# Placing the two operands of the full-width products at agreeing SBUF addresses in a hybrid decoder trunk

## The chip, the cores and the metric

One Trainium2 chip, one of its cores. The time is the device time of one execution of the whole program, in microseconds (us); lower is better. Three runs of the kernel before gave 2153.06, 2153.92 and 2160.28 us, median 2153.92.

## What is computed

The reference is a two-layer decoder trunk over 1024 tokens of width 1024, with 16 learned meta tokens in front (1040 positions). Layer 0 is a state-space mixer with a gated output projection and a mixture of experts (MoE); layer 1 is sliding-window attention over a shared K/V and a second MoE. Everything is in float32.

```python
h = h + s5_mixer(rmsnorm(h), ...)            # ends in z @ w_glu: 1040 x 1024 by 1024 x 2048
h = h + hier_moe(rmsnorm(h), ...)            # 32 experts, each 1024 -> 512 (gate, up) -> 1024 (down)
k, v = split(rmsnorm(h) @ w_kv + b_kv)       # 1024 x 512
q = rmsnorm(h) @ w_q + b_q                   # 1024 x 1024
h = h + (attention(q, k, v, sinks) @ w_o + b_o)
h = h + hier_moe(rmsnorm(h), ...)
return rmsnorm(h)[meta tokens dropped]
```

## The kernel before

**Split products.** A float32 product with a large weight is made of three TensorE products. Each operand is split into a part `hi` (rounded to the fp32r format by ScalarE) and a rest `lo` (VectorE subtracts), and TensorE adds hi x hi, lo x hi and hi x lo into one PSUM bank. One such product has a stationary operand of 128 x 128, loaded by its own LDWEIGHTS, and a moving operand of 128 x 512 that is streamed from SBUF while the next product's stationary operand is being loaded. These are the full-width products of the title. TensorE does them back to back, in five places:

- the mixer's projection, lines 810 to 812 (`products` in `phase_mixer`): four quarters of the weight by nine token tiles by eight chunks by three, 864 products (96 of them for the meta tile, which has 16 stationary columns). Stationary: `z_hi`, `z_lo`. Moving: the weight, `w_hi`, `w_lo`;
- the MoE of each layer, lines 1876 to 1878 (`products` in `phase_moe`): 32 tiles of 128 rows, one per expert here, with 48 products for gate and up and 24 for down, 2304 for each layer. Stationary: `x_hi`, `x_lo`, then `h_hi`, `h_lo`. Moving: the expert's weight in `hi` and `lo`. Between them stand 8 transposes of the gathered rows (`xg`, line 1861) and 4 of the hidden tile (line 1870);
- the K/V/Q projections, line 1094 (`project_pe`): 480 products of 512 columns with the weight stationary and `prj_x_hi`, `prj_x_lo` moving; V is made the other way round, in products of 256 columns, and the meta rows in short ones;
- the output projection of attention, lines 2235 to 2237 (`project` in `phase_attend`): 384 products in bursts of six between the other steps of attention, the last 48 nearly together. Stationary: `o_hi`, `o_lo`. Moving: `wo_hi`, `wo_lo`.

**The order of work.** Each engine runs its own list; semaphores join them. In an MoE layer SP loads three 2 MB weights per expert into six buffers (`raw`), ScalarE makes `hi`, VectorE `lo`, three slots each, and TensorE sends `w_used` when a slot is done. Rows come by an indirect DMA from GpSimd.

|---|---|---|---|
| mixer | `w_hi`, `w_lo`: 128 | `z`: 128, rows of 1040 words, so chunk c lies 64 c further, tokens 64 further | 64, 128, 192, 0, repeated over chunks |
| MoE, layer 0 | `hi` (57568), `lo` (82144): 224 | `x_hi` (157664), `x_lo`, `h_hi`, `h_lo`: 224 | 0 throughout |
| K/V/Q | `prj_x`: 224, rows of 1040 words, so chunk c lies 64 c further | `w_hi`, `w_lo`: 224 | 0, 192, 128, 64, repeated over chunks |
| attention output | `wo_hi`, `wo_lo`: 32 | `o_hi`, `o_lo`: 192 | 160 throughout |
| MoE, layer 1 | `hi` (57568), `lo` (82144): 224 | `x_hi` (154368), `x_lo`, `h_hi`, `h_lo`: 0 | 32 throughout |

The two MoE layers run the same instructions of the same function; the addresses behind the router's tables differ because layer 0 has nine token tiles and layer 1 eight, and layer 0 also holds the biases of the projections.

Of the kernel before, what the change touches and what calls it, by code (L numbers as in the profile page):

```python
# [9 lines left out]
F32R = mybir.dt.float32r  # L10
# [9 lines left out]
SEQ = 1024  # L20
N_META = 16
T_ALL = SEQ + N_META
P = 128
DC = D // P
XT = SEQ // P
# [24 lines left out]
RAW_AT = 229344 - 6 * 8192  # L50
TILE_ORDER = (XT,) + tuple(range(XT))

def tile_rows(i):

    return P if i < XT else N_META
# [33 lines left out]
def phase_mixer(nc, t):  # L90
# [9 lines left out]
    CB = DC  # L100
    NQ = 4
    QW = D // NQ
    BANKS = 6
    RW = G * NCH
    h = t["h"]
    w_glu = t["ssm_w_glu"][0].rearrange("(c p) (v q m) -> p c v q m", c=DC, v=2, q=NQ)
    xm_dram, h_dram, zm_dram = t["xm_dram"], t["h_dram"], t["zm_dram"]
    with ExitStack() as ctx:
        def sb(name, shape, dt=F32):
            return ctx.enter_context(nc.sbuf_tensor("mix_" + name, shape, dt))  # L110

        def region(name, words):

            at = -(-nc.sbuf_base // 32) * 32
            return at, sb(name, [P, words])

        def over(name, shape, at, dt=F32):

            return nc.alloc_sbuf_tensor_at("mix_" + name, shape, dt, offset=at)
# [5 lines left out]

        r1_at, r1 = region("r1", RW)
        v_re, v_im = (r1[:, q * L * JC:(q + 1) * L * JC].rearrange("p (j k c) -> p j k c", k=L, c=C) for q in range(2))
        xm_sq = r1[0:N_META, 0:D]
        st_n = r1[:, :].rearrange("p (a n) -> p a n", n=NCH)

        r2_at, r2 = region("r2", RW)
        xt = r2[:, 0:L * D].rearrange("p (g q c) -> p g q c", g=G, c=C)
        st_a = r2[:, :].rearrange("p (i e a b) -> p i e a b", e=NE, i=BLK, a=8)
        w_raw = r1[:, 0:4 * D].rearrange("p (f c v m) -> p f c v m", f=2, c=DC // 2, v=2)

        r3_at, r3 = region("r3", RW)
        xs = r3[:, 0:L * D].rearrange("p (q d) -> p q d", q=L)
        xm2 = r3[0:2, 0:L * D].rearrange("p (g q c) -> p g q c", g=G, c=C)
        hbuf = r3[0:C, RW // 2:RW // 2 + HB * 4 * HW].rearrange("p (b g m) -> p b g m", b=HB, g=4)
        tm = r3[:, :].rearrange("p (g m) -> p g m", g=G)  # L140

        r4_at, r4 = region("r4", RW)
        sq = r4[:, 0:L * D].rearrange("p (q d) -> p q d", q=L)
        uc = r4[:, :].rearrange("p (g n) -> p g n", g=G)

        s1_at, s1 = region("s1", 4 * D)
        b_raw = s1[:, 0:2 * JC].rearrange("p (x j c) -> p x j c", x=2, c=C)
        c_raw = s1[:, 2 * JC:4 * JC].rearrange("p (x a m) -> p x a m", x=2, m=S)
# [12 lines left out]
        z1 = s1[:, Z0:Z0 + 8 * NCH].rearrange("p (b s n) -> p b s n", b=2, s=4)  # L161
        z_cb = s1[:, Z0 + 8 * NCH:Z0 + 8 * NCH + D].rearrange("p (s g c) -> p s g c", s=L, c=C)

        z_hi, z_lo = (over(f"z_{x}", [P, CB, T_ALL], at, F32R) for x, at in (("hi", r4_at), ("lo", r3_at)))
        HALF = 4 * RW // 2
        w_hi = [over(f"w_hi{b}", [P, DC, 2 * QW], at, F32R) for b, at in enumerate((r2_at, r1_at + HALF))]
        w_lo = [over(f"w_lo{b}", [P, DC, 2 * QW], at, F32R) for b, at in enumerate((r2_at + HALF, s1_at))]
# [72 lines left out]
        def _(sp):  # L240
# [41 lines left out]
            for i in range(NT):  # L282
                n = tile_rows(i)
                src = t["x"][0, i * P:(i + 1) * P, :] if i < XT else t["meta_tokens"]
                sp.dma_start(h[0:n, i, :], src).then_inc(h_in, 16)
# [50 lines left out]
        def _(act):  # L336
# [107 lines left out]
            for q in range(NQ):  # L444
                if q + 1 < NQ:
                    for half in range(2):
                        split_w(q + 1, half)
                if q == 0:
                    act.wait_ge(zm_in, 32)
                    nc.scalar.copy(z_hi[:, :, 0:N_META], zmr[:].rearrange("p b n s -> p b (n s)")).then_inc(zm_hi_done, 1)  # L450
                for i in range(NT):
                    k, n = q * NT + i, tile_rows(i)
                    act.wait_ge(acc_done, k + 1)
                    if k >= 2:
                        act.wait_ge(val_done, k - 1)
                    nc.scalar.activation(sig[0:n, k % 2, :], acc(k)[0:n, QW:2 * QW], ACT.Sigmoid).then_inc(sig_done, 1)

        @block.vector
        def _(dve):
# [201 lines left out]
            for q in range(NQ):  # L661
                if 1 <= q < NQ - 1:
                    for half in range(2):
                        split_w(q + 1, half)
                for i in range(NT):
                    k, n = q * NT + i, tile_rows(i)
                    dve.wait_ge(sig_done, k + 1)
                    if k >= 2:
                        dve.wait_ge(h_done, k - 1)
                    V.tensor_tensor(val[0:n, k % 2, :], acc(k)[0:n, 0:QW], sig[0:n, k % 2, :],  # L670
                                    ALU.mult).then_inc(val_done, 1)
                    dve.wait_ge(val_done, k + 1)
                    hq = h[0:n, i, q * QW:(q + 1) * QW]
                    V.tensor_tensor(hq, hq, val[0:n, k % 2, :], ALU.add).then_inc(h_done, 1)
# [177 lines left out]
KV = N_KV * DH  # L852
NEG = -1e30
SC_W = N_META + 2 * P
TOK = XT * P + N_META
K_META = tuple((3 * m + 1) * P + m * N_META for m in range(3))
K_W = XT * P + len(K_META) * N_META

# [14 lines left out]
def projections(nc, t, sb, sem, ident, mhalf, ss, rstd, ps_x, acc):  # L873
# [18 lines left out]
    bk = sb("prj_bk", [P, K0])  # L892
    bq = sb("prj_bq", [P, DC])
    bv = sb("prj_bv", [P, KV])
    x_at = -(-nc.sbuf_base // 32) * 32
    x_hi, x_lo = (nc.alloc_sbuf_tensor_at(f"prj_x_{x}", [P, DC, TOK], F32R, offset=x_at + q * 4 * DC * TOK)
                  for q, x in enumerate(("hi", "lo")))
    yc = nc.alloc_sbuf_tensor_at("prj_yc", [P, N_YC, 2, D], F32, offset=t["qkv_at"])
    xn = nc.alloc_sbuf_tensor_at("prj_xn", [P, 2, D], F32, offset=t["qkv_end"])
# [21 lines left out]
        return max(k for k, job in enumerate(jobs) if job[0] == (n if n >= K0 else 0)) + 1  # L921

    def split(x, i):
        return x[:, :, i * P:i * P + tile_rows(i)]

    def turned(j):
        return ps_x[j % 2].rearrange("p (c m) -> p c m", c=DC)[:, :, 0:tile_rows(TILE_ORDER[j])]
# [41 lines left out]
    def project_act(act):  # L969
# [15 lines left out]
        def hi_part(j):  # L985
            act.wait_ge(xt_mm, j + 1)
            A.copy(split(x_hi, TILE_ORDER[j]), turned(j)).then_inc(xt_hi, 1)
# [79 lines left out]
    def project_pe(pe):  # L1067
        T = nc.tensor

        def turn(j):  # L1070
            i, n = TILE_ORDER[j], tile_rows(TILE_ORDER[j])
            pe.wait_ge(xn_done, j + 1)
            if j >= 2:
                pe.wait_ge(xt_lo, j - 1)
            for c in range(DC):
                last = T.transpose(ps_x[j % 2][:, c * P:c * P + n],
                                   xn[0:n, j % 2, :].rearrange("p (m c) -> p c m", c=DC)[:, c, :], ident[0:n, 0:n])
            last.then_inc(xt_mm, 1)

        def product(k):  # L1080
            n, at, m = jobs[k]
            if k >= 4:
                pe.wait_ge(acc_free, k - 3)
            for c in range(DC):
                xh, xl = x_hi[:, c, at:at + m], x_lo[:, c, at:at + m]
                if n < K0:
                    wh, wl = w_hi[:, 0:K0, c, :], w_lo[:, 0:K0, c, :]
                    out = acc[k % 4][0:m, 0:KV].rearrange("p (b f) -> p b f", b=K0)
                    pairs = ((xh, wh), (xl, wh), (xh, wl))
                else:  # L1090
                    wh, wl = w_hi[:, n % W_KV, c, :], w_lo[:, n % W_KV, c, :]
                    out, pairs = acc[k % 4][:, 0:m], ((wh, xh), (wh, xl), (wl, xh))
                for s, (stationary, moving) in enumerate(pairs):
                    last = T.matmul(out, stationary, moving, start=(c == 0 and s == 0), stop=(c == DC - 1 and s == 2))
            last.then_inc(acc_done, 1)

        for j in range(NT):
            turn(j)
            if j >= 1 and j < NT - 1:
                pe.wait_ge(xt_lo, j)  # L1100
                product(j - 1)
        for k in range(NT - 2, len(jobs)):
            n, at, m = jobs[k]
            if n < K0:
                pe.wait_ge(xt_lo, NT - 1 if k == NT - 1 else NT)
            elif n >= Q0:
                pe.wait_ge(w_lo_done, n - Q0 + 1)
            product(k)
# [4 lines left out]
def phase_moe(nc, t, layer, out=None):  # L1113
# [27 lines left out]
    with ExitStack() as ctx:  # L1141
        def sb(name, shape, dt=F32):
            return ctx.enter_context(nc.sbuf_tensor(f"moe{layer}_{name}", shape, dt))
# [6 lines left out]
        hi, lo = (sb(x, [P, 3, KC * F], F32R) for x in ("hi", "lo"))  # L1150
# [7 lines left out]
        if not last_layer:  # L1158
            project_sp, project_pool, project_act, project_dve, project_pe = projections(
                nc, t, sb, sem, ident, mhalf, ss, rstd, (ps_xt, ps_y), (ps_g, ps_u, ps_ht, ps_m))  # L1160
# [44 lines left out]
        gi = sb("gi", [P, 1], I32)  # L1205
        unit = sb("unit", [P, 2])
        si = sb("si", [P, 1], I32)
        xg = sb("xg", [P, D])
        x_hi, x_lo = (sb(f"x_{x}", [P, DC, P], F32R) for x in ("hi", "lo"))
        silu = sb("silu", [P, F])  # L1210
# [717 lines left out]
def phase_attend(nc, t):  # L1928
# [16 lines left out]
    with ExitStack() as ctx:  # L1945
        def sb(name, shape, dt=F32):
            return ctx.enter_context(nc.sbuf_tensor("att_" + name, shape, dt))

        def ps(name, shape):
            return ctx.enter_context(nc.psum_tensor("att_" + name, shape, F32))  # L1950
# [6 lines left out]
        own_t = sb("own_t", [P, P])  # L1957
        sinks = sb("sinks", [P, N_HEADS])
        raw = sb("raw", [P, 4, HALF])
        wo_hi, wo_lo = (sb(f"wo_{x}", [P, DC, D], F32R) for x in ("hi", "lo"))  # L1960
        sm = sb("sm", [P, 2, ROW])
        nm = sb("nm", [P, 2, H2])
# [4 lines left out]
        p_own = sb("p_own", [P, 2, H2 * P])  # L1967
        v_step = sb("v_step", [P, 2, KV])
        v_meta = sb("v_meta", [3 * N_META, KV])
        o_hi, o_lo = (sb(f"o_{x}", [P, 2, DC, P], F32R) for x in ("hi", "lo"))  # L1970
        ps_s = ps("ps_s", [P, 4, 512])
        ps_t = ps("ps_t", [P, 2, 512])
# [333 lines left out]
```

## Time and profile before

| | us |
|---|---|
| median of three runs | 2153.92 |
| lowest and highest run | 2153.06, 2160.28 |
| the profiled execution, whole | 2154.48 |
| its span, first to last instruction | 2152.4 |
| TensorE matmuls busy | 1959.0 |
| TensorE weight loads busy | 1573.1 |
| VectorE busy | 1580.2 |
| ScalarE busy | 1251.7 |
| GpSimd busy | 374.3 |
| mean granted TensorE clock, share of full speed | 0.960 |

TensorE is the busiest engine. Its matmuls are pipelined, each being recorded as 0.39 us long while the next begins about 0.23 us after it, so the time of a row of products is read from their starts, not from their durations.

### The profile page before, as it was taken

How to read it: one execution, taken by the hardware profiler on the slowest of the kernel's cores; microseconds unless marked ns; L12 is line 12 of the kernel's file. 1: busy time of each engine (PE TensorE's matmuls, PEld its weight loads, DVE VectorE, ACT ScalarE, POOL GpSimd, SP SyncE). 2: the span in 40 equal slices, each digit the busy share in tenths (PEclk: the TensorE clock that was granted, in tenths of full speed). 3: DMA queues.
4: the chain of work that ended last, by engine and by line, in shares of the span. 5: the costliest groups of instructions: out<-in, count | busy, mean ns of one | idle time of the engine just before them, and what ended most of it. 6: DMA issues, size and time to landing. Idle time of an engine off the chain costs nothing. (4 is left out here: it accounts for less than half of the span.)

```text
span 2152.4 us, 31937 instructions
## 1 busy us (share of the span) xinstructions
PE 1959.0 (91%) x10762; PEld 1573.1 (73%) x10762; DVE 1580.2 (73%) x1767; ACT 1251.7 (58%) x1532; POOL 374.3 (17%) x673
## 2 busy tenths in 40 slices
PE   4959999859999999999699999995899999999991
PEld 3648777748888888888588766664788888888870
DVE  8996321468999999989752376656688888888885
ACT  6614210427777777777530265534577777777771
POOL 1000000401222222221233000003122111122214
PEclk9979999979999999999799999998899999999995
DMA  4174200439999999999612110007599999999976
GB/s 102 26 73 158 91 1 1 169 131 366 385 384 379 380 380 382 383 389 387 230 53 56 46 45 2 1 1 257 189 358 353 374 378 381 386 384 384 381 309 244
DMA packets 136045, 504.69 MB, mean 234 GB/s; under 512 B 38466, under 2 KB 68498, under 8 KB 84754
## 3 DMA queue, kind: packets, MB, share of 16 engines
q1 hardware_dynamic: 114658, 468.71, 59.5%
q0 software_dynamic: 18432, 33.86, 4.1%
q10 hardware_dynamic: 2880, 1.12, 0.4%
q8 instruction: 47, 0.77, 0.2%
q14 instruction: 28, 0.23, 0.0%
HBM read 488.47 MB, written 47.32 MB: 249 GB/s over the span
## 5 line engine op out<-in xcount | busy, mean ns | idle before, releaser
L1713 DVE TENSOR_TENSOR moe_lo<-moe_raw,moe_hi 128x2048 fp32r<-128x2048 f32 x378 | 860.8, 2291 | 102.4 <-ACT moe_hi L1488 99.3
L1488 ACT CAST moe_hi<-moe_raw 128x2048 fp32r<-128x2048 f32 x374 | 712.9, 1915 | 139.8 <-PE moe_ps_g L1878 67.0
L1876 PE MATMUL moe_ps_g<-moe_hi,moe_x_hi 128*128 128x512 f32 x512 | 209.0, 408 | 4.9 <-DVE moe_lo L1713 3.0
L1876 PE MATMUL moe_ps_y<-moe_hi,moe_h_hi 128*128 128x512 f32 x512 | 207.0, 404 | 3.8 <-DVE moe_h_lo L1729 3.8
L1878 PE MATMUL moe_ps_g<-moe_lo,moe_x_hi 128*128 128x512 f32 x512 | 203.0, 396 | 0.0
L1877 PE MATMUL moe_ps_g<-moe_hi,moe_x_lo 128*128 128x512 f32 x512 | 202.7, 396 | 0.0
L1878 PE MATMUL moe_ps_y<-moe_lo,moe_h_hi 128*128 128x512 f32 x512 | 202.0, 395 | 0.0
L1877 PE MATMUL moe_ps_y<-moe_hi,moe_h_lo 128*128 128x512 f32 x512 | 201.8, 394 | 0.0
L1878 PE MATMUL moe_ps_u<-moe_lo,moe_x_hi 128*128 128x512 f32 x512 | 201.2, 393 | 0.0
L1876 PE MATMUL moe_ps_u<-moe_hi,moe_x_hi 128*128 128x512 f32 x512 | 200.8, 392 | 0.0
L1877 PE MATMUL moe_ps_u<-moe_hi,moe_x_lo 128*128 128x512 f32 x512 | 200.8, 392 | 0.0
L1495 ACT CAST moe_x_hi<-moe_ps_xt 128x1024 fp32r<-128x1024 f32 x62 | 63.0, 1015 | 114.7 <-PE moe_ps_xt L1861 114.7
L1876 PEld LDWEIGHTS moe_ps_g<-moe_hi,moe_x_hi 128*128 128x128 f32 x512 | 98.3, 192 | 25.1 <-DVE moe_lo L1713 3.4
L1876 PEld LDWEIGHTS moe_ps_y<-moe_hi,moe_h_hi 128*128 128x128 f32 x512 | 96.7, 189 | 23.5 <-DVE moe_lo L1713 4.1
L1878 PEld LDWEIGHTS moe_ps_g<-moe_lo,moe_x_hi 128*128 128x128 f32 x512 | 97.3, 190 | 22.6
L1878 PEld LDWEIGHTS moe_ps_y<-moe_lo,moe_h_hi 128*128 128x128 f32 x512 | 96.6, 189 | 22.1
L1877 PEld LDWEIGHTS moe_ps_g<-moe_hi,moe_x_lo 128*128 128x128 f32 x512 | 97.7, 191 | 19.6
L1878 PEld LDWEIGHTS moe_ps_u<-moe_lo,moe_x_hi 128*128 128x128 f32 x512 | 96.1, 188 | 21.6
L1876 PEld LDWEIGHTS moe_ps_u<-moe_hi,moe_x_hi 128*128 128x128 f32 x512 | 96.1, 188 | 21.6
L1877 PEld LDWEIGHTS moe_ps_u<-moe_hi,moe_x_lo 128*128 128x128 f32 x512 | 96.1, 188 | 21.6
L1405 POOL COPY moe_si<-moe_idx_out 128x1 int32 x64 | 49.9, 779 | 353.9 <-ACT moe_y L1508 353.9
L1877 PEld LDWEIGHTS moe_ps_y<-moe_hi,moe_h_lo 128*128 128x128 f32 x512 | 96.8, 189 | 19.5
(463 smaller groups left out, 3745.3 us busy)
## 6 DMA issues: line engine op xcount, KB each, us to landing
moe_raw<-moe_w_gate SPq DMA_DIRECT2D x128, 1024.0 KB, 6.9
moe_raw<-moe_w_up SPq DMA_DIRECT2D x128, 1024.0 KB, 7.9
moe_raw<-moe_w_down SPq DMA_DIRECT2D x128, 1024.0 KB, 7.4
mix_r<-ssm_w_glu SPq DMA_DIRECT2D x16, 512.0 KB, 5.4
xn_dram<-moe_work SPq DMA_DIRECT2D x16, 512.0 KB, 6.4
prj_yc<-y_dram SPq DMA_DIRECT2D x8, 1024.0 KB, 7.0
moe_raw<-y_dram SPq DMA_DIRECT2D x8, 1024.0 KB, 11.7
mix_r<-x SPq DMA_DIRECT2D x8, 512.0 KB, 5.3
```

Of the source, the lines that this page charges most:

```text
L1405: G_.tensor_copy(dst[:, :], idx[:, bass.ds(tile, 1)]).then_inc(ix_step, 1)
L1488: A.copy(hi[:, slot(number, k), :], raw[:, k, :]).then_inc(hi_done, 1)
L1495: A.copy(x_hi[:, :, :].rearrange("p c m -> p (c m)"), ps_xt[:, :]).then_inc(xt_hi, 1)
L1713: V.tensor_tensor(lo[:, slot, :], raw[:, k, :], hi[:, slot, :].bitcast(F32), ALU.subtract).then_inc(lo_done, 1)
L1876: T.matmul(out, x_h, w_h, start=first, stop=False)
L1877: T.matmul(out, x_l, w_h, start=False, stop=False)
L1878: return T.matmul(out, x_h, w_l, start=False, stop=final)
```

## The change

No instruction is added, removed or reordered. Only addresses change.

- `aligned(base, like)` gives the next address at or above `base` that is a multiple of 32 and, if `like` is given, agrees with it modulo 256. `lead` declares an unused tile of so many words that the next tile begins at such an address.
- Mixer: each row of `z_hi` and `z_lo` gets 48 unused words in front (`Z_PAD`), so that rows are 1088 words (17 x 256 bytes) apart and the tokens begin at 128 modulo 256, as the weights do. The regions under them grow by 1536 bytes each. The meta columns (16 of them, before the tokens) then lie 64 below the weights modulo 256 in every chunk.
- K/V/Q: `prj_x_hi` and `prj_x_lo` keep 1024 token columns; the 16 meta columns move to tiles of their own. Their start is made to agree with `RAW_AT` (224), where it already is.
- MoE: `xg` is led to the residue of `t["qkv_at"]`, 224. In layer 0 that skips nothing; in layer 1 it skips 224 bytes, and `xg`, `x_hi`, `x_lo`, `silu`, `hid`, `h_hi`, `h_lo` and `y` all move from 0 to 224.
- Attention: `o_hi` and `o_lo` move by 96 bytes, from 192 to 32.

```diff
+def aligned(base, like=None):
+    at = -(-base // 32) * 32
+    return at if like is None else at + (like - at) % 256
+
+def lead(nc, sb, like):
+    skip = aligned(nc.sbuf_base, like) - aligned(nc.sbuf_base)
+    if skip:
+        sb("lead", [P, skip // 4])
...
+    Z_PAD = 48
...
+        sb("r3_more", [P, CB * Z_PAD])
         r4_at, r4 = region("r4", RW)
...
+        sb("r4_more", [P, CB * Z_PAD])
         s1_at, s1 = region("s1", 4 * D)
...
-        z_hi, z_lo = (over(f"z_{x}", [P, CB, T_ALL], at, F32R) for x, at in (("hi", r4_at), ("lo", r3_at)))
+        z_hi, z_lo = (over(f"z_{x}", [P, CB, Z_PAD + T_ALL], at, F32R)[:, :, Z_PAD:]
+                      for x, at in (("hi", r4_at), ("lo", r3_at)))
...
-    x_at = -(-nc.sbuf_base // 32) * 32
-    x_hi, x_lo = (nc.alloc_sbuf_tensor_at(f"prj_x_{x}", [P, DC, TOK], F32R, offset=x_at + q * 4 * DC * TOK)
+    x_at = aligned(nc.sbuf_base, RAW_AT)
+    m_at = x_at + 2 * 4 * DC * SEQ
+    x_hi, x_lo = ((nc.alloc_sbuf_tensor_at(f"prj_x_{x}", [P, DC, SEQ], F32R, offset=x_at + q * 4 * DC * SEQ),
+                   nc.alloc_sbuf_tensor_at(f"prj_xm_{x}", [P, DC, N_META], F32R, offset=m_at + q * 4 * DC * N_META))
                   for q, x in enumerate(("hi", "lo")))
...
-                xh, xl = x_hi[:, c, at:at + m], x_lo[:, c, at:at + m]
+                xh, xl = columns(x_hi, c, at, m), columns(x_lo, c, at, m)
...
         si = sb("si", [P, 1], I32)
+        lead(nc, sb, t["qkv_at"])
         xg = sb("xg", [P, D])
...
+        wo_at = aligned(nc.sbuf_base)
         wo_hi, wo_lo = (sb(f"wo_{x}", [P, DC, D], F32R) for x in ("hi", "lo"))
...
+        lead(nc, sb, wo_at)
         o_hi, o_lo = (sb(f"o_{x}", [P, 2, DC, P], F32R) for x in ("hi", "lo"))
```

## Rows read from the trace of the kernel before

**Rows 1.** Windows view, one stage each: us, busy us (x instructions) by engine, PEclk, DMA share, GB/s

```profile
196.00:398.00 202.00, 201.33 (x885) 154.00 (x883) 47.50 (x82) 30.94 (x52) 0.00 (x0) 1.00 0.17 56
464.00:1037.00 573.00, 566.16 (x2660) 473.93 (x2661) 508.62 (x288) 446.85 (x318) 117.67 (x214) 0.99 0.96 367
1094.00:1216.00 122.00, 121.15 (x572) 99.95 (x570) 33.18 (x55) 8.42 (x8) 35.04 (x16) 1.00 0.16 44
1247.00:1455.00 208.00, 206.06 (x1444) 133.34 (x1442) 131.47 (x469) 106.15 (x449) 9.96 (x53) 1.00 0.03 9
1515.00:2105.50 590.50, 583.98 (x2680) 478.22 (x2680) 506.78 (x285) 448.68 (x317) 114.65 (x215) 0.99 0.93 354
```

**Rows 2.** Waits view of TensorE, 1510 to 2106 us, longest: total us, times, longest us

```profile
PE moe_ps_ht L1870 <- DVE moe_hid L1725: 3.0, 1, 3.0
```

**Rows 3.** Waits view of all engines, layer 0's MoE, 520 to 1030 us

```profile
DVE moe_lo L1713 <- ACT moe_hi L1488: 34.6, 87, 0.4
ACT moe_hi L1488 <- PE moe_ps_y L1878: 23.4, 29, 0.8
```

**Rows 4.** Timeline view of TensorE: start us, us; eight transposes, layer 0, 27 tiles apart

```profile
530.74 1.04 PE L1861 MATMUL moe_ps_xt<-moe_ident,moe_xg 128*128 128x128 f32 x8
...
1010.08 1.04 PE L1861 MATMUL moe_ps_xt<-moe_ident,moe_xg 128*128 128x128 f32 x8
```

**Rows 5.** Timeline view of TensorE, the same transposes in layer 1, 27 tiles apart

```profile
1582.83 1.05 PE L1861 MATMUL moe_ps_xt<-moe_ident,moe_xg 128*128 128x128 f32 x8
...
2073.25 1.05 PE L1861 MATMUL moe_ps_xt<-moe_ident,moe_xg 128*128 128x128 f32 x8
```

**Rows 6.** Timeline view of TensorE, layer 0: two products of "up", twelve apart

```profile
915.86 0.39 PE L1876 MATMUL moe_ps_u<-moe_hi,moe_x_hi 128*128 128x512 f32 x1
...
918.58 0.39 PE L1876 MATMUL moe_ps_u<-moe_hi,moe_x_hi 128*128 128x512 f32 x1
```

**Rows 7.** Timeline view of TensorE, layer 1: two products of "up", twelve apart

```profile
1813.36 0.40 PE L1876 MATMUL moe_ps_u<-moe_hi,moe_x_hi 128*128 128x512 f32 x1
...
1816.16 0.40 PE L1876 MATMUL moe_ps_u<-moe_hi,moe_x_hi 128*128 128x512 f32 x1
```

**Rows 8.** Timeline view of TensorE, the mixer's projection: one pass over four chunks

```profile
353.05 0.40 PE L810 MATMUL mix_pst<-mix_w_hi,mix_z_hi 128*128 128x512 f32 x1
...
355.13 0.40 PE L810 MATMUL mix_pst<-mix_w_hi,mix_z_hi 128*128 128x512 f32 x1
355.37 0.39 PE L811 MATMUL mix_pst<-mix_w_hi,mix_z_lo 128*128 128x512 f32 x1
...
355.83 0.40 PE L810 MATMUL mix_pst<-mix_w_hi,mix_z_hi 128*128 128x512 f32 x1
```

**Rows 9.** Timeline view of TensorE, K/V/Q: two products, twelve apart

```profile
1131.59 0.39 PE L1094 MATMUL moe_ps_g<-prj_x_hi,w_hi 128*128 128x512 f32 x1
...
1134.37 0.39 PE L1094 MATMUL moe_ps_g<-prj_x_hi,w_hi 128*128 128x512 f32 x1
```

**Rows 10.** Timeline view of TensorE, attention: four intervals inside a burst of six

```profile
1325.04 0.39 PE L2236 MATMUL att_ps_y<-att_wo_hi,att_o_lo 128*128 128x512 f32 x1
...
1325.97 0.40 PE L2237 MATMUL att_ps_y<-att_wo_lo,att_o_hi 128*128 128x512 f32 x1
```

**Rows 11.** Timeline view of TensorE, attention's last half projection, 23 intervals

```profile
1448.93 0.39 PE L2235 MATMUL att_ps_s<-att_wo_hi,att_o_hi 128*128 128x512 f32 x1
...
1454.30 0.39 PE L2237 MATMUL att_ps_s<-att_wo_lo,att_o_hi 128*128 128x512 f32 x1
```

**Rows 12.** Timeline view of TensorE, layer 0: second to eighth product behind transposes

```profile
910.62 0.39 PE L1877 MATMUL moe_ps_g<-moe_hi,moe_x_lo 128*128 128x512 f32 x1
...
912.01 0.39 PE L1877 MATMUL moe_ps_g<-moe_hi,moe_x_lo 128*128 128x512 f32 x1
```

**Rows 13.** Timeline view of TensorE, layer 0: five products at the start of "down"

```profile
904.67 0.39 PE L1877 MATMUL moe_ps_y<-moe_hi,moe_h_lo 128*128 128x512 f32 x1
...
905.60 0.39 PE L1878 MATMUL moe_ps_y<-moe_lo,moe_h_hi 128*128 128x512 f32 x1
```

More of the change, by code:

```diff
@@ L854 @@
 SC_W = N_META + 2 * P
-TOK = XT * P + N_META
 K_META = tuple((3 * m + 1) * P + m * N_META for m in range(3))
@@ L923, in split, with columns @@
     def split(x, i):
-        return x[:, :, i * P:i * P + tile_rows(i)]
+        return x[0][:, :, i * P:(i + 1) * P] if i < XT else x[1][:, :, :]
+    def columns(x, c, at, m):
+        return x[0][:, c, at:at + m] if at < XT * P else x[1][:, c, :]
     def turned(j):
```

## The prediction

> **What bounds the kernel now.** I read the windows view by stage first. In the five stages that hold full-width products TensorE is busy for 201.33 of 202, 566.16 of 573, 121.15 of 122, 206.06 of 208 and 583.98 of 590.5 us; no other engine comes near except VectorE in the MoE layers (508.62 and 506.78) [rows 1]. The waits view says the same from the other side: in all of layer 1's MoE the longest wait of TensorE is one of 3.0 us at the start [rows 2], while in layer 0's steady part TensorE has none; there ScalarE waits 29 times for TensorE to give a slot back, and VectorE for ScalarE [rows 3]. No engine waits for a weight transfer. So these stages, about 1,695 us of the 2152.4, end when TensorE's list ends, and the list's length is the number of products times the interval between their starts. The change alters no instruction, so the whole question is that interval. The timeline's starts give it; durations do not.
>
> **The interval depends on the addresses.** The kernel before holds a comparison of its own: the same function runs as two MoE layers. The instructions and the tile sizes are the same; what differs is that the stationary operands agree with the moving ones modulo 256 bytes in layer 0 and lie 32 bytes off in layer 1. From one tile's transposes to those 27 tiles later layer 0 takes 1010.08 - 530.74 = 479.34 us, 17.753 a tile [rows 4]; layer 1 takes 2073.25 - 1582.83 = 490.42, 18.164 a tile [rows 5]. Inside a tile, twelve products of "up" take 2.72 us in layer 0, 226.7 ns each [rows 6], and 2.80 us in layer 1, 233.3 ns each [rows 7]. The clock is granted in full in both. The gap of 6.6 ns on 72 products would be 0.48 us a tile; the tiles differ by 0.41, because in layer 0 the first products behind the transposes are not yet at the low interval: six intervals take 1.39 us, 231.7 each [rows 12], so 6 x 5.0 ns twice a tile, 0.06 us, are not gained.
>
> The other stages fit. The mixer, whose difference walks through 64, 128, 192, 0, takes 2.78 us for twelve, 231.7 each [rows 8]; K/V/Q, which walks the other way, 2.78 as well [rows 9]. Attention's last run, 160 off throughout, takes 5.37 us for 23, 233.5 each [rows 11]. So a difference that merely stays the same doesn't bring 226.7 (32 and 160 don't); of the constant ones seen, only 0 does. What I can't see is a stage with difference 0 on residues other than 224, or whether 0 in the mixer and K/V/Q does what it does in the MoE.
>
> The Trainium skill speaks against the change: "SBUF — State Buffer", "Who interferes with whom", gives TensorE two independent read ports, one for the moving operand and one for weight loads, and says that TensorE waits for nobody. By that rule addresses would make no difference, and the sum would be zero. The trace doesn't agree, with 17.753 against 18.164 us for one and the same list.
>
> **The change, part by part.**
>
> *MoE, layer 1.* The lead of 224 bytes puts its stationary operands where layer 0 has theirs modulo 256. I take layer 0's time for it: 32 tiles x (18.164 - 17.753) = 13.1 us. Bounds: 0, if the difference between the layers isn't the address, and 32 x 72 x 6.6 ns = 15.2 us, if the slow start behind the transposes went too. What would be late next is the feed (ScalarE's `hi`, VectorE's `lo`, the weight transfers), and layer 0 already runs it at 17.753 with TensorE never waiting [rows 1, 3, 4]. Its DMA share is 0.96 against 0.93, so there is little room below that pace, but none is needed.
>
> *Mixer.* 768 of the 864 products come to difference 0. At 231.7 - 226.7 = 5.0 ns each that is 3.8 us. The four meta tiles stay off (by 192) and I leave their 96 products at today's interval; behind each, six intervals of relocking as in rows 12 cost 0.03 us, 0.1 in all. I take 3.7 us, bounds 0 and 864 x 5.0 ns = 4.3. Nothing else there is near TensorE's 201.33 us: VectorE has 47.50 and ScalarE 30.94 [rows 1].
>
> *K/V/Q.* 480 products of 512 columns x 5.0 ns = 2.4 us, less 0.1 for restarts behind the short meta products: 2.3. The 256-column products of V and the meta products I leave as they are; if V's 192 moved by 5 ns either way, it would be 1.0 us. GpSimd's 35.04 us in 122 leaves it ahead [rows 1].
>
> *Attention.* The bursts of six are too short: four intervals inside one take 0.93 us [rows 10], and layer 0's four at the same place behind transposes, with difference 0, take 0.93 too [rows 13]. Only the nearly continuous end gains: some 40 intervals x (233.5 - 226.7) = 0.3 us. Bounds 0 and, if the 56 bursts ran at 226.7 at once, 56 x 4 x 5.8 ns = 1.3 us more.
>
> *Layer 0's MoE, the copies, the DMAs.* `xg` doesn't move in layer 0. ScalarE's and VectorE's writes of `z` and `prj_x` go to rows a little further apart or closer, and no row shows such a step to cost anything; if it did, their idle time in these stages would hide it. The unused tiles are neither written nor read. All other tiles of the mixer move by 1536 or 3072 bytes, multiples of 256. I take nothing.
>
> Sum: 13.1 + 3.7 + 2.3 + 0.3 = 19.4 us. The profiled execution took 2154.48 us, 2.08 more than its span, so 2135.1; the median lies 0.56 below that execution, so 2134.5.
>
> **What else moves.** Stages begin up to 19 us earlier, and with them the stretches at half clock between stages. The two MoE layers lose about a hundredth of their time to such stretches (PEclk 0.99) [rows 1], some 6 us each, and the three runs differ by up to 7.2 us. One such stretch more or less is about 3 us. I put +-4 us on the median for it.
>
> **Rivals.**
>
> *Only layer 1's MoE gains.* Agreement modulo 256 might be enough only with residue 224, or only in an order of operands as in the MoE; mixer and K/V/Q would go on at 231.7. For it: no row shows them at difference 0 for long, and the mixer has agreeing products that still take long (next rival). 2134.5 + 6.3 = 2140.8.
>
> *The layers differ for another reason.* A loop that is paced by something else, the transfers for instance, would show the same two periods, and the skill's rule on the two ports leads here. Against it: TensorE doesn't wait, and the mixer and K/V/Q differ from both within one loop, chunk by chunk. No change, 2153.9.
>
> *Agreement is the collision.* If two streams that start on the same residue meet in the same part of the memory, agreeing is the worst case, and layer 0 escapes it only by a fixed lag. In the mixer the interval from 355.13 to 355.37, where a moving operand at 128 meets the load of a stationary one at 128, is 240 ns by the timeline, longer than its neighbours [rows 8]. The place would be the mixer's and K/V/Q's lists, which have no gap in which such a lag could form. If every agreeing product took some 236 ns (240 as printed, in steps of 10, over the 231.7 mean), mixer and K/V/Q would lose 1,248 x 4.3 ns = 5.4 us, and layer 1, if caught as well, 2304 x 2.7 ns = 6.2 us: 2165.5. It decides once agreeing products average over 233.3 ns in layer 1; layer 0, all agreeing, averages 226.7 [rows 6], which speaks strongly against it.
>
> **How the numbers follow.** Forecast as summed: 0.78, with its own range 2130.5 to 2138.5. Only layer 1: 0.11. No difference: 0.06. Slower by collision: 0.05. The range reaches from 2130, where the meta tiles, attention's bursts and V also gain, to 2143, which takes in the second case with a half-clock stretch on top. A difference under 0.3%, about 6.5 us, is what a measurement can't tell from none. Faster by more than that: 0.88; within it: 0.07; slower: 0.05.
>
> **What would show it.** In the profile after, twelve products of "up" in layer 1 should take 2.72 us and its tiles 17.75; twelve in the mixer and in K/V/Q 2.72 instead of 2.78, with the meta tiles unchanged; attention's last 23 intervals 5.21 instead of 5.37; layer 0 nothing. The forecast is wrong if layer 1 still takes 18.16 (the reason isn't the address), if TensorE begins to wait in it (the feed bounds), or if the mixer's intervals stay mixed (agreement isn't enough).

## The result, and the profile after

The median went from 2155.19 us (2153.06 to 2160.28, four runs) to 2137.44 us (2136.98 to 2138.15, four runs): ratio 0.9913, 95% interval 0.9897 to 0.9930. A second comparison of the same two kernels gave 2155.73 and 2138.82 us (2137.52 to 2142.09), ratio 0.9924, 0.9904 to 0.9943. The forecast was 2134.5, its range 2130 to 2143. The profiled execution of the kernel after took 2138.15 us and has a span of 2136.2, 16.2 less than before. In its line numbers the mixer's products are 827 to 829, K/V/Q's 1115, the MoE's 1898 to 1900 with the transposes on 1883, attention's 2259 to 2261.

Windows view of the kernel after, the five stages (us, busy us and instructions of PE, PEld, DVE, ACT and POOL, PEclk, DMA share, GB/s); it answers to [rows 1]:

```profile
195.70:394.40 198.70, 197.99 (x887) 154.14 (x885) 47.52 (x82) 31.13 (x52) 0.00 (x0) 1.00 0.17 57
462.00:1035.00 573.00, 566.60 (x2662) 474.50 (x2662) 508.32 (x287) 447.11 (x317) 117.24 (x213) 0.99 0.96 367
1092.00:1213.60 121.60, 120.45 (x571) 101.20 (x570) 32.91 (x55) 8.41 (x8) 34.89 (x16) 0.99 0.16 44
1245.00:1451.20 206.20, 204.32 (x1436) 133.16 (x1436) 130.83 (x468) 105.30 (x447) 9.89 (x53) 1.00 0.03 9
1511.00:2089.50 578.50, 571.74 (x2679) 478.20 (x2677) 506.15 (x284) 446.80 (x317) 120.78 (x215) 0.99 0.94 361
```

The mixer's window is 3.3 us shorter and layer 1's 12.0, with the work in them as before. TensorE still fills every window; the other engines' busy times are the same within 2 us, apart from GpSimd's 6 us more in layer 1.

Timeline view of TensorE, the kernel after (start us, duration us, line, operation): eight transposes in layer 1, 27 tiles apart, as [rows 5]; two products of "up" in layer 1, twelve apart, as [rows 7]:

```profile
1576.69 1.04 PE L1883 MATMUL moe_ps_xt<-moe_ident,moe_xg 128*128 128x128 f32 x8
...
2056.03 1.04 PE L1883 MATMUL moe_ps_xt<-moe_ident,moe_xg 128*128 128x128 f32 x8
...
1802.71 0.39 PE L1898 MATMUL moe_ps_u<-moe_hi,moe_x_hi 128*128 128x512 f32 x1
...
1805.43 0.39 PE L1898 MATMUL moe_ps_u<-moe_hi,moe_x_hi 128*128 128x512 f32 x1
```

27 tiles take 479.34 us, 17.753 each, layer 0's period to the last digit [rows 4]; twelve products take 2.72 us, 226.7 ns each.

The same view in the mixer (two products of a token tile, twelve apart, as [rows 8]; then two of the meta tile, 16 stationary columns, twelve apart), in K/V/Q (as [rows 9]) and over attention's last 23 intervals (as [rows 11]):

```profile
350.33 0.39 PE L827 MATMUL mix_pst<-mix_w_hi,mix_z_hi 128*128 128x512 f32 x1
...
353.05 0.39 PE L827 MATMUL mix_pst<-mix_w_hi,mix_z_hi 128*128 128x512 f32 x1
...
241.21 0.40 PE L827 MATMUL mix_psr<-mix_w_hi,mix_z_hi 128*16 128x512 f32 x1
...
243.99 0.40 PE L827 MATMUL mix_psr<-mix_w_hi,mix_z_hi 128*16 128x512 f32 x1
...
1127.74 0.39 PE L1115 MATMUL moe_ps_m<-prj_x_hi,w_lo 128*128 128x512 f32 x1
...
1130.46 0.39 PE L1115 MATMUL moe_ps_m<-prj_x_hi,w_lo 128*128 128x512 f32 x1
...
1445.36 0.39 PE L2259 MATMUL att_ps_s<-att_wo_hi,att_o_hi 128*128 128x512 f32 x1
...
1450.58 0.39 PE L2261 MATMUL att_ps_s<-att_wo_lo,att_o_hi 128*128 128x512 f32 x1
```

Mixer and K/V/Q now take 2.72 us for twelve instead of 2.78; attention 5.22 for 23 instead of 5.37; the meta tile stays at 2.78.

Where the 16.2 us are. Each stage is measured from the start of its first product or transpose to the start of its last, before against after; "second" is the profile of the same kernel in the second comparison (span 2135.8). Rounding leaves 0.1 in a column:

| | forecast | after | second |
|---|---|---|---|
| mixer | -3.7 | -3.5 | -3.5 |
| MoE, layer 0 | 0 | +0.2 | +0.2 |
| K/V/Q | -2.3 | -0.3 | -0.4 |
| attention | -0.3 | -1.0 | -1.0 |
| MoE, layer 1 | -13.1 | -11.6 | -14.1 |
| between the stages | 0 | -0.1 | +2.1 |
| sum | -19.4 | -16.2 | -16.7 |

Two terms fell short, K/V/Q and, in the first profile, layer 1. In both places there is a stretch at half clock inside the list of products. Timeline view of TensorE, the kernel after, K/V/Q behind K's 24 short meta products:

```profile
1109.50 0.26 PE L1115 MATMUL moe_ps_m<-prj_xm_hi,w_lo 128*128 128x16 f32 x1
1109.62 0.30 PE L1115 MATMUL moe_ps_m<-prj_xm_hi,w_hi 128*128 128x16 f32 x1
...
1111.19 0.63 PE L1115 MATMUL moe_ps_g<-prj_x_hi,w_lo 128*128 128x512 f32 x1
1111.62 0.63 PE L1115 MATMUL moe_ps_g<-prj_x_hi,w_hi 128*128 128x512 f32 x1
```

Windows view of TensorE (us, busy us and instructions, PEclk, DMA share, GB/s): the kernel after, at that place and in the last tile of layer 1:

```profile
1109.70:1113.10 3.40, 3.40 (x11) 0.50 0.35 104
1113.10:1116.50 3.40, 3.40 (x16) 1.00 0.17 51
...
2078.00:2082.50 4.50, 2.58 (x14) 1.00 0.00 0
2082.50:2085.90 3.40, 3.40 (x10) 0.50 0.16 58
```

The kernel before, at K/V/Q's place, and the kernel after in its second profile, at layer 1's:

```profile
1109.40:1112.80 3.40, 3.40 (x29) 1.00 0.05 12
1112.80:1116.20 3.40, 3.40 (x17) 1.00 0.53 154
```

```profile
2078.40:2081.80 3.40, 2.60 (x14) 1.00 0.00 0
2081.80:2085.20 3.40, 2.27 (x10) 1.00 0.03 10
2085.20:2088.60 3.40, 3.40 (x16) 1.00 0.11 43
```

Full-width products stand 0.43 us apart instead of 0.227: 3.4 us at 1.2 GHz instead of 2.4 do the work of 1.7. Of the 2.0 us that K/V/Q misses, list by list, 1.6 are this stretch. The lists with V's 192 products of 256 columns are 0.2 longer than before, and so is the list of V's short meta products ahead of them, which differs by more than that from run to run. The 480 products of 512 columns themselves give back what was forecast: where no stretch stands in them, their four lists take 108.93 us against 111.24 before, 2.3 less (run "walk" below).

Layer 1 misses 1.5 us in the first profile, where its last tile holds such a stretch. The second profile has none there, and its 14.1 exceeds the term because the stretch near the start of the layer is 3.4 us long (granted clock 0.50 from 1529.8 to 1533.2 us) instead of 6.8 (before, from 1531.5 to 1538.3).

### The profile page after: what moved, and what is told of

The parts are those of the page before. It is cut to its first block and busy times, and to the rows that moved or that the text cites. A ratio compares the mean times of both kernels' runs of the same rounds, so it can differ in the third digit from the quotient of the medians.

```text
span 2136.2 us, 31937 instructions
## 1 busy us (share of the span) xinstructions
PE 1941.3 (91%) x10762; PEld 1575.1 (74%) x10762; DVE 1580.2 (74%) x1767; ACT 1249.3 (58%) x1532; POOL 376.4 (18%) x673
## 6 DMA issues: line engine op xcount, KB each, us to landing
moe_raw<-y_dram SPq DMA_DIRECT2D x8, 1024.0 KB, 11.6
```

## The experiments

Intervals below are means of start-to-start times of full-width products at full clock, more than ten products behind the last other instruction, without the few over 300 ns, unless rows are shown. Runs given with one time are single runs; what they show is read from their intervals, not from that time.

**Which half does what.** The kernel before with nothing but layer 1's lead:

```diff
+        lead(nc, sb, t["qkv_at"])
         xg = sb("xg", [P, D])
```

> The kernel before with one part of the change: the 224 bytes of lead in layer 1's MoE. Theory (agreement modulo 256 sets the interval): a tile of layer 1 takes 17.75 us instead of 18.16, twelve products of 'up' 2.72 instead of 2.80, the mixer and K/V/Q stay at 2.78, and the time is 13 us below before (ratio 0.994). Rival 'another reason' (the two MoE layers differ for something other than the address): no change, ratio 1.000.

Measured: 2145.25 us against 2157.8, ratio 0.9944 (0.9925 to 0.9963). Timeline view of TensorE in this run, layer 1's transposes 27 tiles apart, then its waits view for the layer (total us, times, longest us):

```profile
1580.62 1.04 PE L1875 MATMUL moe_ps_xt<-moe_ident,moe_xg 128*128 128x128 f32 x8
...
2064.30 1.04 PE L1875 MATMUL moe_ps_xt<-moe_ident,moe_xg 128*128 128x128 f32 x8
```

```profile
PE moe_ps_xt L1875 <- DMA moe_xg<-xn_dram,moe_gi: 2.2, 1, 2.2
```

The 483.68 us hold one late gather of rows: two tiles took 18.01 and 21.83 us, 4.34 more than their neighbours, with a half-clock stretch behind the wait of 2.2. The rest is 479.34 again, 17.75 a tile. All other stages are as before. So 224 bytes of unused words give layer 1 its whole gain per tile.

The counterpart is the changed kernel without that lead:

```diff
-        lead(nc, sb, t["qkv_at"])
         xg = sb("xg", [P, D])
```

> The changed kernel without its lead in layer 1's MoE, so only mixer, K/V/Q and attention are placed. Theory: twelve products take 2.72 us in the mixer and in K/V/Q, a tile of layer 1 still 18.16, and the time is 6 us below before (ratio 0.997). Rival 'only layer 1 gains': the mixer and K/V/Q stay at 2.78 and the time is that of before.

Measured: 2150.88 us, ratio 0.9969 (0.9959 to 0.9979); layer 1's tiles at 18.163. Timeline view of TensorE in this run, layer 1, 27 tiles apart:

```profile
1577.50 1.05 PE L1882 MATMUL moe_ps_xt<-moe_ident,moe_xg 128*128 128x128 f32 x8
...
2067.91 1.05 PE L1882 MATMUL moe_ps_xt<-moe_ident,moe_xg 128*128 128x128 f32 x8
```

0.9944 x 0.9969 = 0.9913, the ratio of the whole change: the parts add up.

**Other differences.** The changed kernel with each stage's stationary operands moved against the moving ones. The first three use steps of 32 bytes or 16, in all stages; for the MoE:

```diff
-        x_hi, x_lo = (sb(f"x_{x}", [P, DC, P], F32R) for x in ("hi", "lo"))
+        x_hi, x_lo = placed("x_hi", DC, (64, 96)[layer]), placed("x_lo", DC, (64, 96)[layer])
```

where `placed` puts a tile at `qkv_at` plus so many bytes, modulo 256.

> The changed kernel with other constant differences (stationary minus moving, modulo 256): mixer, K/V/Q and attention 128; MoE layer 0: 64 for gate and up, 128 for down; MoE layer 1: 96 for gate and up, 192 for down. Theory (only 0 is fast): twelve products take 2.77 to 2.80 us everywhere, layer 0's tile goes from 17.75 to about 18.16, and the time is 10 to 16 us above before. Rival A (any constant difference that is a multiple of 64 is as good as 0, so that agreement modulo 64 is enough): 2.72 us for twelve in the mixer, K/V/Q, layer 0 and the down products of layer 1, 2.80 only for layer 1's gate and up; the time is about 10 us below before.

> As the last one, with differences of 64 in the mixer, K/V/Q and attention; MoE layer 0: 16 for gate and up, 160 for down; MoE layer 1: 224 (32 below) for gate and up, 32 for down. Theory (only 0 is fast): all intervals 231 to 235 ns, with 16 the only open case, since half a line of 32 bytes may or may not be enough of a shift; the time is 10 to 16 us above before. Rival A: the mixer and K/V/Q at 2.72 us for twelve, the MoE layers at 2.80.

> The changed kernel with differences of 192 in the mixer and K/V/Q and 224 in attention. In MoE layer 0 only x_lo is moved by 128 (hi, lo and x_hi still agree), in MoE layer 1 only lo is moved by 128 (x_hi, x_lo, h_hi, h_lo agree with hi). Theory: the interval is set by whichever pair meets, so one mismatched product in three is enough to lose most of the gain in gate and up: 229 to 232 ns on average in both layers, while down in layer 0, whose operands all agree, stays at 227. The mixer and K/V/Q at 192 show whether the 229.5 ns that 192 gave for layer 1's down products belongs to the difference (then 229.5 again) or to that list (then 232 to 233). Rival (each product by itself): one in three at 232 and two at 227, 228.5 on average.

Measured: 2164.0, 2173.65 and 2150.2 us, beside 2157.8, 2157.8 and 2159.88 of the kernel before. The first lies 6 us above its kernel before, where 10 to 16 were expected: 192 and, in part, 128 cost less than the rest. The intervals of all these runs stand in the table below. Timeline view of TensorE, two products twelve apart: first run, "up" in layer 1 at 96; second run, the mixer's meta tile at 0; third run, the mixer at 192:

```profile
1713.57 0.39 PE L1906 MATMUL moe_ps_u<-moe_hi,moe_x_hi 128*128 128x512 f32 x1
...
1716.38 0.40 PE L1906 MATMUL moe_ps_u<-moe_hi,moe_x_hi 128*128 128x512 f32 x1
```

```profile
242.13 0.40 PE L827 MATMUL mix_psr<-mix_w_hi,mix_z_hi 128*16 128x512 f32 x1
...
244.91 0.40 PE L827 MATMUL mix_psr<-mix_w_hi,mix_z_hi 128*16 128x512 f32 x1
```

```profile
299.94 0.39 PE L827 MATMUL mix_psr<-mix_w_hi,mix_z_hi 128*128 128x512 f32 x1
...
302.69 0.39 PE L827 MATMUL mix_psr<-mix_w_hi,mix_z_hi 128*128 128x512 f32 x1
```

2.81 us for twelve at 96; 2.78 for the meta tile although its operands now agree (230.7 ns on average against 231.3 in the kernel after), so short stationary operands gain next to nothing from it; 2.75 at 192, halfway. In the third run only `x_lo` (layer 0) or only the moving `lo` (layer 1) was off by 128. From the start of `hi` with `x_hi`, `hi` with `x_lo` and `lo` with `x_hi` to the next start it is 232.5, 234.2 and 226.7 ns in layer 0 and 232.7, 231.0 and 229.8 in layer 1. The first product of each three meets its partner in agreement and takes 232.5 and more; in layer 1 the second does too and takes 231.0. So, as the theory had it, a disagreeing operand can slow its neighbours in the list, though not every one: `lo` with `x_hi` in layer 0 keeps 226.7. The averages, 231.0 to 231.2, leave the rival's 228.5 out.

**How exact.** Finer steps in the MoE, the same edit with `(8, 240)` for `x` and `(4, 252)` for `h`:

> The changed kernel with differences of a few words in the MoE layers: layer 0 8 bytes for gate and up, 4 for down; layer 1 240 (16 below) for gate and up, 252 (4 below) for down. 16 gave 233.4 ns where 0 gives 227.0. Theory (two streams that must stay a fixed lag apart, in steps of a word): even 4 bytes cost something, 230 ns or more. Rival (what counts is the line of 32 bytes that is read, and 16 was simply too near its edge): 4 and 8 bytes are as good as 0, 227 ns. Mixer, K/V/Q and attention as in the changed kernel, 226.7.

Measured: 2149.76 us. Timeline view of TensorE in this run, "up" twelve apart in layer 0 (8 above), then in layer 1 (240, that is 16 below):

```profile
902.35 0.39 PE L1906 MATMUL moe_ps_u<-moe_hi,moe_x_hi 128*128 128x512 f32 x1
...
905.11 0.39 PE L1906 MATMUL moe_ps_u<-moe_hi,moe_x_hi 128*128 128x512 f32 x1
...
1705.49 0.39 PE L1906 MATMUL moe_ps_u<-moe_hi,moe_x_hi 128*128 128x512 f32 x1
...
1708.21 0.39 PE L1906 MATMUL moe_ps_u<-moe_hi,moe_x_hi 128*128 128x512 f32 x1
```

2.76 and 2.72 us. The rival fell, and with it the line of 32 bytes, of which no run shows a sign: 4 bytes off cost nearly the full price (232.5 ns above, 233.1 below). The theory held there and at 8, but it had no place for 240: 16 below costs nothing. Two more runs looked at its surroundings, with `(232, 208)` and `(236, 240)`, then `(248, 176)` and `(244, 200)`:

> Changed kernel with other differences (stationary minus moving, modulo 256) in the MoE layers, to find how wide the good place just below agreement is. Layer 0: x 232 (24 below), h 236 (20 below). Layer 1: x 208 (48 below), h 240 (16 below). Known so far: 0 and 240 on x give 226.7 to 227.1 ns, 252 on h 233.2, 8 on x 230.9, 224 233.3, 192 about 229, other values 229.5 to 234.3. Theory 1 (240 is a second good place in itself, whatever the operand): h in layer 1 comes to 227 ns, x at 232 and h at 236 lie at 229 to 233 ns, x at 208 at 231 to 234. Theory 2 (240 was good only for x, in the up and gate products of layer 1): h at 240 gives 230 ns or more. Theory 3 (a wide good range from 232 to 244): all three of 232, 236 and 240 give 227. I expect theory 1; total 2146 to 2152.

> As the run before with other differences again. Layer 0: x 248 (8 below), h 244 (12 below). Layer 1: x 176 (80 below), h 200 (56 below). If only 0, 16 below and in part 64 below are good, all four differences lie at 229 to 234 ns and the tiles at 18.0 to 18.2 us in both layers: total 2152 to 2158. If everything from 16 below to 8 below is good, x in layer 0 gives 227 and its tiles 17.9. I expect the first.

Measured: 2153.51 and 2154.98 us. `h` at 240 took 226.7 ns where every other value took 230.0 or more: 240 is a second good place, for `x` and for `h`, and a narrow one. That is theory 1, and in the second run the first of its two expectations. All constant differences that were seen:

| stationary minus moving, modulo 256 | interval, ns |
|---|---|
| 0 | 226.6 to 227.1 |
| 4; 8; 16 | 232.5; 230.6; 233.1 |
| 32; 64; 96 | 233.3 to 233.4; 233.3; 234.2 |
| 128; 160 | 232.4 to 233.2; 233.2 to 233.7 |
| 176; 192; 200 | 230.0; 228.9 to 229.3; 230.3 |
| 208; 224; 232; 236 | 233.3; 233.3; 231.1; 231.5 |
| 240 | 226.7 |
| 244; 248; 252 | 233.3; 233.3; 233.1 |

The residue itself doesn't matter: 32 (attention), 128 (mixer) and 224 (MoE, K/V/Q) all reach 226.7 at difference 0. Nor do larger steps: in the changed mixer rows of `z` are 4352 bytes apart and rows of the weight 2048, so the full difference grows by 9 x 256 bytes a chunk, and the interval stays at 226.7, while 128 costs.

All this holds for products of 512 columns. V's products, 256 columns with `prj_x` stationary, behave otherwise. Timeline view of TensorE, two of them 24 apart, in the kernel after (difference 0), then in the third run (64 here, since `prj_x` is the stationary operand):

```profile
1097.45 0.28 PE L1115 MATMUL moe_ps_g<-w_lo,prj_x_hi 128*128 128x256 f32 x1
...
1100.33 0.28 PE L1115 MATMUL moe_ps_u<-w_lo,prj_x_hi 128*128 128x256 f32 x1
```

```profile
1101.13 0.28 PE L1115 MATMUL moe_ps_g<-w_lo,prj_x_hi 128*128 128x256 f32 x1
...
1103.85 0.28 PE L1115 MATMUL moe_ps_u<-w_lo,prj_x_hi 128*128 128x256 f32 x1
```

2.88 against 2.72 us. Over all of V's uninterrupted intervals the means are 119.6 ns at 0, 119.4 at 128, 116.2 at 192 and 114.4 at 64, and 118.0 in the kernel before, where the difference walks. Agreement is the worst of these for V, hardly different from 128, and the change cost it 1.6 ns a product.

**Which pair must agree.** The load of the next stationary operand runs beside the stream of the present one, so "agree" can mean a product's own pair, or the load and the stream beside it. In the mixer both were let walk by 32 bytes a chunk, own pairs always agreeing:

```diff
-        w_hi = [over(f"w_hi{b}", [P, DC, 2 * QW], at, F32R) for b, at in enumerate((r2_at, r1_at + HALF))]
+        w_hi = [over(f"w_hi{b}", [P, DC, 2 * QW + 8], at, F32R) for b, at in enumerate((r2_at, r1_at + HALF))]
```

and likewise `w_lo` and `z`, whose rows become 1032 words.

> The changed kernel with another layout in the mixer alone: rows of z are 4128 bytes apart and rows of the weights 2080, so that both walk by 32 bytes from chunk to chunk and a product's own two operands always agree modulo 256, while the stationary operand of the first product of a chunk is 32 away from the moving operand of the last product of the chunk before, during which it is loaded. Theory A (what must agree is a product's own pair): 226.7 ns on average, 2.72 us for twelve. Theory B (what must agree is the operand being loaded and the one being streamed at that time): one interval in three meets a difference of 32, so 229 to 232 ns on average, 2.75 to 2.78 for twelve.

Measured: 2140.21 us; intervals of 229, 233 and 231 ns in turn, 230.8 on average. I took that for theory B, which makes a counterpart: `w_lo` 32 bytes further, so that every load agrees with the stream beside it and every third own pair doesn't.

> Counterpart of the run in which the mixer's rows walk by 32 bytes a chunk: the same kernel with the mixer's w_lo moved 32 bytes further. Now the third product of each chunk (z_hi with w_lo) has its own pair 32 bytes apart, while the load of the next chunk's z_hi, which runs beside the stream of w_lo, agrees with it modulo 256. Everything else as in the changed kernel. Theory A (a product's own two operands must agree): one product in three is off, so the mixer's late intervals average at or above the 230.9 ns of the walk, and the mixer's 768 token products take 1 to 3 us more than the changed kernel's 175.07. Theory B (the load and the stream that run at the same time must agree): late intervals of 226.7 ns, 768 products in 175.0 to 175.4 us, total within 2 us of the changed kernel. I expect B.

Measured: 2142.07 us; the mixer's list, 201.2 us before and 197.7 after, took 200.8 in the walk and 202.0 in its counterpart, whose intervals average 232.4 ns. Timeline view of TensorE, two products twelve apart, in the walk and in its counterpart:

```profile
250.65 0.39 PE L828 MATMUL mix_psr<-mix_w_hi,mix_z_hi 128*128 128x512 f32 x1
...
253.43 0.39 PE L828 MATMUL mix_pst<-mix_w_hi,mix_z_hi 128*128 128x512 f32 x1
```

```profile
250.70 0.40 PE L828 MATMUL mix_psr<-mix_w_hi,mix_z_hi 128*128 128x512 f32 x1
...
253.49 0.40 PE L828 MATMUL mix_pst<-mix_w_hi,mix_z_hi 128*128 128x512 f32 x1
```

2.78 and 2.79 us, where A had forecast 2.72 for the walk and B the same for its counterpart. So B fell as well as A: neither agreement alone suffices. Apart from difference 240, low intervals were seen only where both hold, and in both walks the residue of the moving starts steps as well. Whether the step itself costs, or each of the two disagreements, these two runs can't tell, since a stream on another residue than the last can't agree with both.

**Longer bursts in attention.** The projection of the tile before was called every second step with twice the products, to see whether bursts of twelve would reach 226.7:

```diff
-                    project(i - 1, c // 4, (2 * (c % 4), 2 * (c % 4) + 1))
+                    if c % 2:
+                        project(i - 1, c // 4, range(2 * (c % 4) - 2, 2 * (c % 4) + 2))
```

> The changed kernel with attention's output projection issued in bursts of twelve products at every second step instead of six at every step; same products, same waits. Each burst pays about 0.09 us at its first product (316 ns against 227), some 0.1 us at its last, and 5 ns for each of its first intervals, so 28 bursts fewer would save 28 x 0.2 = 5.6 us if nothing else becomes late. Rival: in the steps without a burst TensorE waits for ScalarE and VectorE (0.2 us or more each), and the time is the same or longer than that of the changed kernel.

Measured: 2160.95 us, so the rival of the expectation came true: attention's list is 21.8 us longer than in the changed kernel. Nor did the bursts reach 226.7: their seventh to eleventh intervals take 230.4 ns on average. Waits view of this run, 1210 to 1460 us, two of TensorE's longest:

```profile
PEld att_ps_o L2239 <- ACT att_pt L2096: 33.3, 27, 1.5
PE att_ps_o L2239 <- DVE att_o_lo L2163: 23.7, 28, 1.2
```

In the kernel after TensorE doesn't wait for `att_pt` at all and for `o_lo` only 0.7 us, once. Its bursts of six fill the time in which ScalarE and VectorE make these two, which is worth far more than a few ns a product.

**Does the shortfall belong to the change?** The changed kernel again:

> The changed kernel once more, unaltered, in its own comparison with the kernel before. Ratio 0.991, with the profiled execution telling which half-clock stretches come back. If the stretch behind K's short meta products (1109.7 to 1113.1 us in the first profile) and the one in the last tiles of layer 1 (2082.5 to 2085.9) belong to the changed kernel, both stand in this profile too and the sum stays 16 to 17 us. If they are chance, one or both are missing and the span is 1.5 to 3 us shorter, 2133 to 2135. I expect the K/V/Q one to be there again and the other to be uncertain.

Measured: 2138.82 us, ratio 0.9924; layer 1 without its stretch, 14.1 us faster than before; K/V/Q with a stretch again, at 1123.6 to 1127.0. The total hardly moved, because what lies between the stages came out 2.2 us longer in sum than in the first profile. Over all 14 profiles a stretch inside K/V/Q stands in six of the nine whose K/V/Q operands agree and in one of the five others; every kernel has the same short meta products there. That is too few to call it a cause: it stays open. In the three of the nine without one (the walk and the last two runs with other differences in the MoE), the list and the gap ahead of it are together 1.2 to 1.8 us shorter than before, against 0.4 in the kernel after: the stretch accounts for the larger part of what the term missed.

## Why the prediction was right, by its own steps

*What bounds.* Right: TensorE fills all five stages before and after, and its list got shorter by the intervals alone.

*The interval depends on the addresses, by layer 0 against layer 1.* Right, and shown: one unused tile takes layer 1's period from 18.164 to 17.753. What inside the chip makes it so no run shows. The rule of the Trainium skill weighed there ("SBUF — State Buffer", "Who interferes with whom") would have left it at 18.164.

*MoE, layer 1, 13.1 us.* The tile period is exact. The term came out at 11.6 and 14.1 in two profiles, for stretches at half clock: the first has one more in its last tile, the second a shorter one near its start.

*Mixer, 3.7.* 3.5, with 231.3 to 226.7 ns on the token tiles: the price of 231.7 from twelve printed starts was 0.4 ns high. The meta tiles stayed at 231.3, as forecast, and for another reason than the text gave: at difference 0 they take 230.7, hardly less.

*K/V/Q, 2.3.* Right for the 480 products (231.7 to 226.7 ns, 2.3 us where no stretch stands), mis-sized for the stage: 0.3 to 0.4 came. The text had no stretch in this list (1.6 us) and left V's products unchanged, with 1.0 us as the price of 5 ns; they went up by 1.6 ns, because agreement doesn't help them.

*Attention, 0.3.* Under-sized: 1.0. The step that failed is "four intervals take 0.93 in layer 0 too". Printed in hundredths, that row could not show 234.0 against 230.9 ns, which the bursts gained; the bound of 1.3 more for them held.

*The +-4 us for stretches at half clock.* This carried the error: 19.4 was forecast and 16.2 to 16.7 came. That the total still fell near the forecast is in part luck, since where such stretches stand changes from run to run. The prices in the text were too high: one of 3.4 us costs 1.7 in a dense list, not 3, and the 6.8 us near the start of each MoE layer cost at most 3.4, not 6.

*The rivals.* "Only layer 1 gains" fell with the run that leaves layer 1 out and is still 0.31% faster. "Another reason" fell with the run that moves layer 1 alone. "Agreement is the collision" fell: 226.7 at three residues. The 240 ns interval in [rows 8] stands in a list whose difference walks; the intervals at that place of the three average 234.0 before and 226.7 after.

## What to carry to other kernels

Where TensorE's list bounds a stage, measure the interval between starts of equal products, not their durations, and compare it between places that run the same code; two layers that differ only in where the allocator put things are a free experiment. If the intervals differ, lay the stationary and the moving tiles so that their starts agree modulo 256 bytes and stay on one residue from chunk to chunk; a few unused words do it, and nearly agreeing (4 bytes off) is hardly better than not agreeing. This was measured for fp32 products of 128 x 128 by 128 x 512 with one weight load each, on one core; products of 256 columns got slower by it and those of 16 stationary columns hardly changed, so measure each shape. Expect 2 to 3% of the list's time at best, and read what stretches at half clock take back before you blame the mechanism.

## What had not been expected of the hardware

- The interval isn't a smooth function of the difference: 226.7 ns at 0 and at 240, 229 at 192, 230 at 176 and 200, and 231 to 234 elsewhere, with 244 to 252, between the two good places, at 233.
- Both the load beside a stream and a product's own pair count: with either off by 32 bytes once in three products, all three slow down, to 230.8 and 232.4 ns on average.
- A stationary operand of 16 columns takes 230.7 ns at difference 0 and 231.3 at 192.
- Products of 256 columns take 119.6 ns at difference 0 and 114.4 at 64: what is best for 512 columns is the worst of the four differences seen for them.
- One gather that came 2.2 us late cost 4.3 us in all, with the half-clock stretch behind it.
